# Gates of the latent projection two slots earlier, row slots planned by last use, dots moved between stages, and routing's last turns placed between value groups

## The reference

```python
h = modulate(rmsnorm(x, norm_w), shift, scale)
q, k, v, xr, yr = split(h @ w_in, 5 parts of 512)
att = neighbourhood_attention(q, k, v, k_ctx, v_ctx, rpb)      # latent; context: plain attention
xc  = centred_depthwise_conv(xr)                               # width 4
r, i = sigmoid(xc @ w_a + b_a), sigmoid(xc @ w_i + b_i)        # for each of two directions
a   = exp(8 * r * log_sigmoid(lam)); b = sqrt(1 - a*a) * (i * xc)
rg  = (scan_forward(a, b) + scan_backward(a, b)) * gelu(yr)    # RG-LRU
x   = x + gate_mix * (concat(att, rg) @ w_out)
h2  = modulate(rmsnorm(x, norm_ffn_w), shift2, scale2)
s   = (h2 @ w_q) . sub_keys            # 8 heads, two halves, 128 keys each
expert, g = top 16 of 16 x 16 candidates, softmax of their scores   # 128 (head, place) pairs a token
y   = sum over the 128: g * gelu(h2 . u[expert]) * v[expert]   # u, v: 16384 x 1024
out = rmsnorm(x + gate_ffn * y)
```

## Time and profile before

| | us |
|---|---|
| median of 3 executions | 3422.59 (3416.72 to 3429.27) |
| the profiled execution | 3423.91 |
| its span (first to last instruction) | 3422.1 |
| mean granted clock of PE | 0.962 |
| busy: PE, DVE, ACT, POOL | 3087.1, 2666.0, 1050.5, 1966.8 |
| latent projection | 358 to 652.5 |
| latent attention | 652.5 to 869.9 |
| latent output projection | 869.9 to 1024.8 |
| latent routing | 1024.8 to 1420.5 |
| place_weights | 1420.5 to 1637 |
| experts | 1637 to 3422 |

### The profile page before, as it was taken

How to read it: one execution, slowest core, us unless ns; L and a number is a source line. 1 busy time by engine, 2 the same in 40 slices (tenths; PEclk the granted TensorE clock), 3 DMA queues, 4 the chain that set the end, 5 groups by cost and what they waited for, 6 DMA issues and landing times.

```text
span 3422.1 us, 46361 instructions
## 1 busy us (share of the span) xinstructions
PE 3087.1 (90%) x15031; PEld 2030.5 (59%) x15031; DVE 2666.0 (78%) x5959; ACT 1050.5 (31%) x1886; POOL 1966.8 (57%) x1674
## 2 busy tenths in 40 slices
PE   6879899689899998677599999999999999999996
PEld 4647345456455444366365677776777766767774
DVE  2328788798577999699699788887878778877888
ACT  4731234366111111388211222222222222222222
POOL 0000466455335566453488777777777777777771
PEclk9989999799999999799799999999999999999998
DMA  9432688766867888799999999999999999999997
GB/s 338 167 110 95 215 267 277 233 213 219 321 227 259 297 290 303 272 337 390 343 366 384 411 412 412 412 411 411 412 411 412 411 411 411 412 412 412 411 412 303
DMA packets 374297, 1131.15 MB, mean 331 GB/s; under 512 B 32968, under 2 KB 99784, under 8 KB 374016
## 3 DMA queue, kind: packets, MB, share of 16 engines
q0 software_dynamic: 221184, 805.40, 62.0%
q1 hardware_dynamic: 144464, 316.41, 24.4%
q10 hardware_dynamic: 8496, 7.44, 0.7%
HBM read 1075.93 MB, written 53.19 MB: 330 GB/s over the span
## 4 chain that ended last, share of the span: by engine, by line
PE 23%; DMA 13%; POOL 6%; issue 6%; DVE 3%; ACT 0%; POOLq 0%; SPq 0%; DVEq 0%; ACTq 0%
DMA exp_value_row<-in_v_rows,exp_v_id 11%; PE exp_a_ps L2502 10%; PE exp_o_ps L2530 7%; PE exp_v_ps L2486 4%; POOL exp_value_row L2654 2%; PE exp_o_ps L2535 2%; POOL exp_more_row L2643 1%; POOL edge_u_raw L2643 1%; POOL edge_row L2643 1%; DMA exp_value_row<-in_u_rows,edge_id_and_dot 1%; DVE edge_u_raw L2708 0%; POOL exp_value_row L2643 0%; DMA exp_final_row<-scratch_x 0%; DVE exp_v_lo L2672 0%; DMA exp_out<-in_u_rows,edge_id_and_dot 0%
## 5 line engine op out<-in xcount | busy, mean ns | idle before, releaser
L403 POOL DMA_INDIRECT ahead_row<-in_u_rows,keep_tables x256 | 338.1, 1321 | 656.1 <-POOLq L102 364.1
L2654 POOL DMA_INDIRECT exp_value_row<-in_v_rows,exp_v_id x448 | 487.8, 1089 | 166.1 <-issue 136.0
L2502 PE MATMUL exp_a_ps<-exp_xT_hi,exp_u_hi 128*128 128x512 f32 x1024 | 411.0, 401 | 29.2 <-DVE exp_u_lo L2672 22.7
L2502 PE MATMUL exp_a_ps<-exp_xT_lo,exp_u_hi 128*128 128x512 f32 x1024 | 401.2, 392 | 0.0
L2502 PE MATMUL exp_a_ps<-exp_xT_hi,exp_u_lo 128*128 128x512 f32 x1024 | 400.3, 391 | 0.0
L413 DVE CUSTOM_DVE_ANT_0 ahead_row<-ahead_row,ahead_x 128x1024 f32<-128x1024 f32 x256 | 305.2, 1218 | 85.0 <-DMA ahead_row<-in_u_rows,keep_tables 84.5
L2789 DVE TENSOR_TENSOR keep_acc<-exp_o_ps,keep_acc 128x1024 f32<-128x1024 f32 x250 | 304.7, 1219 | 70.5 <-PE exp_o_ps L2530 53.1
L2585 ACT ACTIVATE exp_hidden<-exp_a_ps 128x512 f32<-128x512 f32 x128 | 76.6, 598 | 920.1 <-PE exp_a_ps L2502 920.1
L2643 POOL DMA_INDIRECT edge_row<-in_u_rows,edge_id_and_dot x224 | 292.8, 1307 | 103.1 <-POOL exp_v_id L2629 42.5
L2530 PE MATMUL exp_o_ps<-exp_v_hi,exp_w_hi 128*128 128x512 f32 x896 | 286.8, 401 | 5.1 <-DVE keep_acc L2838 5.1
L2530 PE MATMUL exp_o_ps<-exp_v_lo,exp_w_hi 128*128 128x512 f32 x896 | 281.7, 395 | 0.0
(11 more groups left out here) (446 smaller groups left out, 6230.3 us busy)
## 6 DMA issues: line engine op xcount, KB each, us to landing
exp_u_raw<-in_uT SPq DMA_DIRECT2D x126, 512.0 KB, 6.7
exp_v_raw<-in_v_rows SPq DMA_DIRECT2D x112, 512.0 KB, 6.7
exp_g_raw<-scratch_g SPq DMA_DIRECT2D x64, 512.0 KB, 7.9
scratch_g<-place_grid SPq DMA_DIRECT2D x3, 8192.0 KB, 51.1
proj_ctx_mod_slab<-in_w_mod SPq DMA_DIRECT2D x8, 2048.0 KB, 11.7
heads_early_room<-in_w_in SPq DMA_DIRECT2D x10, 1024.0 KB, 10.7
mod_slab<-in_w_mod SPq DMA_DIRECT2D x4, 2048.0 KB, 20.3
queries_slab<-in_w_q SPq DMA_DIRECT2D x4, 2048.0 KB, 24.5
```

Source lines behind the costliest of these rows:

```text
L403: nc.gpsimd.indirect_dma_start(out=ahead.row[:, n % KEY_RING, :], out_offset=None, in_=io["u_rows"], in_offset=bass.IndirectOffsetOnAxis(a ...
L2502: mm = nc.tensor.matmul(a_ps[e][:, :], u[part][:, e, k, :], xT[xp][:, k, :], start=(k == 0 and part == 0 and xp == 0), stop=(k == KD - 1 a ...
L2654: nc.gpsimd.indirect_dma_start(out=value_row[:, 4 * (j % 2) + t, :], out_offset=None, in_=io["v_rows"].rearrange("a b n -> (a b) n"), in_o ...
```

## The change

1. **Row slots.** `Ahead.rows` plans the slot of each row: the one whose last use is longest ago, of 4, or of up to 8 where more room is lent. In the projection two more rows lie in the parts of `v` that are filled last, for the first 104 units; in the output projection four more lie in `keep["acc"]`. `gather_keys` waits for the dot that last used the slot.
2. **Gates.** In the latent projection tile ct's gates begin at turn `FIRST_SLOT` = 6 (slot 6 of slab ct) instead of turn 8. PE and ACT follow one list of turns. ACT waits for dot 104 ahead of its V copy 4, the first into the lent room. ACT makes two of the four tiles of hT, DVE the other two.
3. **Dots.** Projection 136 gathers and 132 dots (8 first, then 3, 1, 4, 1, 1, 2 a direction), attention 64 gathers and 68 dots, output projection 56 dots (15 first, then 6 + 4 + 4).
4. **Bias.** SP loads pairs 0 and 1 at the end of the projection, when the last tile is done; in the attention it loads the context's values first and then pairs 2 and 3. 28 gathers stand ahead of the middle memsets, 40 before.
5. **Routing.** In the latent group's, two value groups, then the turns of one h2 tile, four times; one group; the identifiers' turns; the last three groups. h2 is turned into `q_ps[2]` and `q_ps[3]` and copied in halves. ACT's last `values_out` goes to the end, SP's second `values_store` behind the stores of h2.

The diff, cut to its core:

```diff
@@ class Ahead
+    def rows(self, units, more=(), until=0):
+        places = [self.row[:, n, :] for n in range(KEY_RING)] + list(more)
...
+        for at, n in enumerate(units):
+            usable = range(len(places) if at < until else KEY_RING)
+            s = min(usable, key=lambda p: last_use.get(p, -1))
...
+            if s in last_use:
+                self.freed_by[n] = last_use[s] + 1
+            last_use[s] = n
@@ def gather_keys
-    if n >= KEY_RING:
-        pool.wait_ge(ahead.dots, n - KEY_RING + 1)
+    row, landed = ahead.slot[n]
+    if n in ahead.freed_by:
+        pool.wait_ge(ahead.dots, ahead.freed_by[n])
@@ def projection_and_rg_lru
+    FIRST_SLOT = SLOTS_PER_SLAB if front is None else 2 * FRONT_TILES + 2
+    def tile_at(turn):
+        ct, step = divmod(turn - FIRST_SLOT, SLOTS_PER_SLAB)
+        return (ct, step) if 0 <= ct < RG_TILES else (None, None)
...
+        WIDE_DOTS = WIDE_RING_DOTS if units else 0
+        if units:
+            ahead.rows(units, [v[:, t:t + 2, :].rearrange("p i n -> p (i n)") for t in range(2 * FRONT_TILES, TILES_G, 2)], WIDE_DOTS)
...
+            if not context:
+                sp.wait_ge(tile_done, RG_TILES)
+                for q in range(EARLY_BIAS):
+                    load_bias(io, sp, early, bias_tiles(fused), q)
...
-                    if a:
-                        gate_products(a - 1, slot)
+                    gate_products(*tile_at(SLOTS_PER_SLAB * a + slot))
...
+                    if WIDE_DOTS and u == 2 * FRONT_TILES:
+                        act.wait_ge(ahead.dots, WIDE_DOTS)
...
+            for turn in range(0 if front is None else 2 * FRONT_TILES, SLOTS_PER_SLAB * (SLABS + 1)):
+                a, slot = divmod(turn, SLOTS_PER_SLAB)
+                ct, step = tile_at(turn)
+                gate_step(ct, step)
+                if a < SLABS:
+                    copy_features(a, slot)
+                else:
+                    copy_v(a, slot)
+                if step == SLOTS_PER_SLAB - 1:
+                    gelu(ct)
+            if not context:
+                act.wait_ge(tile_done, RG_TILES)
+                act.wait_ge(v_made, V_UNITS)
+                nc.scalar.activation(hT[:, 6:8, g.at:g.at + NT], fused[:, Y0 + 2:Y0 + 4, :], ACT.Copy)
...
-            dots_left = list(units)
+            dots_left = list(units[:-CARRIED_DOTS])
...
-                    dots(2)
+                    dots(3)
...
-                    dots(3)
+                    dots(4)
...
-            nc.vector.tensor_copy(hT[:, 4:8, g.at:g.at + NT], fused[:, Y0:Y0 + 4, :])
-DOTS_FIRST = 16
+            by_dve = 4 if context else 2
+            nc.vector.tensor_copy(hT[:, 4:4 + by_dve, g.at:g.at + NT], fused[:, Y0:Y0 + by_dve, :])
+DOTS_FIRST = 8
+CARRIED_DOTS = KEY_RING
+WIDE_RING_DOTS = 104
@@ def attention
-                for q in range(PAIRS):
-                    for half in range(2):
-                        sp.dma_start(bias[half * 64:half * 64 + 64, 2 * q:2 * q + 2, half:half + 15, :],
-                                     io["rel_bias"][:, 2 * q:2 * q + 2, :, :]).then_inc(bias_in[q], 16)
-                    if q == 0:
-                        sp.dma_start(v_ctx[:, :, :], io["v_ctx"].rearrange("l p n -> p l n")).then_inc(v_in, 16)
+                sp.dma_start(v_ctx[:, :, :], io["v_ctx"].rearrange("l p n -> p l n")).then_inc(v_in, 16)
+                for q in range(EARLY_BIAS, PAIRS):
+                    load_bias(io, sp, early, bias, q)
...
+                MIDDLE = len(units) // 2 - len(carried)
+                first_half, second_half = units[:MIDDLE], units[MIDDLE:]
@@ def out_projection
+            ahead.rows(units, [keep["acc"][:, n, :] for n in range(MORE_ROWS)], len(units))
...
-                    dots(5)
+                    dots(6)
...
-                        dots(3)
+                        dots(4)
@@ def routing
+        turned_ps = [h_ps[:, half * SLAB:(half + 1) * SLAB] if context else q_ps[2 + half] for half in range(2)]
...
+                values_store(val, sp, 0, scratch["ffn"][CTX.first])
             if not context:
                 for i in range(NG):
                     sp.wait_ge(h2_ready, i + 1)
                     sp.dma_start(scratch["h2"][i], h2[:, i % 2, :]).then_inc(h2_out[i % 2], 16)
+                values_store(val, sp, 1, scratch["ffn"][CTX.first + 1])
...
-            values(len(values_left))
-            if val:
-                pe.wait_ge(val.out_ready, CONTEXT_GATHER)
+            pe.wait_ge(q_ready, 4 * sum(len(parts_of(a)) for a in range(SLABS)))
             for i, t in enumerate(GATHERED):
                 if i:
                     pe.wait_ge(h2_ready, i)
+                values(2)
...
+            values(1)
...
             last.then_inc(ids_turned, 1)
+            values(len(values_left))
...
+            if val:
+                values_out(nc, val, act, 1, h_ps)
-PROJECTION_DOTS, ATTENTION_DOTS = 128, 80
+PROJECTION_DOTS, ATTENTION_DOTS = 136, 64
```

142 lines of the change are left out of this document (79 added, 63 removed).

## The result

The changed kernel takes 3404.28 us, median of 6 (3401.17 to 3407.83), against 3422.14 of the kernel before, median of 6 (3416.72 to 3429.27): a ratio of 0.9948, 95% interval 0.9935 to 0.996. That is 17.9 us less, where 33.5 were forecast; the time lies 0.7 us inside the upper end of the stated range. The profiled execution of the changed kernel took 3401.17 us, its span is 3399.4.

The account below looks back on a forecast made before the run. Experts were taken as DMA-bound, the latent stages as bound by their hand-overs. Projection -13.0, attention -11, output projection +1.5 and routing -11 gave -33.5: 3423.9 to 3390.4 us, by the median 3389; range 3378 to 3405.

Parts of the forecast that it names:

- The projection's work: Latent projection: earlier gates and six rows let DVE finish before PE; last copy at 639.1, 13.0 us less.
- Rival B: Latent projection: rows stay late, so the stage gains 5.2 us instead of 13.0; total 3397 us, chance 0.14.
- D: Projection rival: POOL gathers only between DVE's operations; total about 3421 us, slower from 2.32 dots a gather; chance 0.04.
- The projection's end: Hand-over to the attention: SP's wait for tile 3 and four bias loads cost nothing.
- The attention: Latent attention: bias waits 6.2, clock 3 and DVE-bound steps 2 give 11 us less; bounds 5 and 17.
- The bias waits: Attention's first steps: loading bias pairs 0 and 1 early removes waits of 4.75 and 1.45 us, 6.2 less.
- The clock: Attention's first four steps: a shorter PE pause keeps its clock up, 3 us less; range 0 to 7.6.
- The 12 steps bound by DVE: Attention after its first four steps: fewer dots give 0.2 us a step until PE takes over, 2 us less.
- the ring: Output projection: eight rows put four more gathers beside w_out, 0.4 us more; bounds 0 and 5.
- the dots: Output projection: eight more dots lie in DVE's slack, but one more precedes the last reciprocal, 1.1 us more.
- Routing: Latent routing: h2 turns and identifiers fit into PE's waits for gathers, 11 us less; bounds 8 and 14.
- Rival C: Small terms fail together: attention gains 8, routing 8, output projection loses 5; 3399.9 us, by the median 3399; chance 0.11.

Follow-up runs that it names:

- e9: Changed kernel with the latent projection's gates starting at turn 8 as before the change: projection 301.49 us against 288.10.
- e8: Changed kernel with four rows in the projection's ring throughout and no ACT wait for dot 104: projection 313.17 us against 288.10; execution 3427.88 us.
- e5: e2 with no row gathered in the projection for the attention (132 gathers there, 68 in the attention): projection 281.55 us, execution 3391.16 us.
- e2: Changed kernel with only bias pair 0 loaded early, after tile 1, and pairs 1 to 3 in the attention: projection 287.87 us against 288.10.
- e1: Changed kernel with all four bias pairs loaded in the attention, in the earlier order: projection 280.55 us against 288.10, attention 216.53 against 211.73.
- e7: Changed kernel with the attention's dots two, then three (six steps), then two a step, none in the last: attention 207.43 us against 211.73.
- e6: Changed kernel with the output projection's four more rows used only from its 16th gather on: output projection 155.05 us against 159.60.
- e10: Changed kernel with routing's order, turns and copies of the kernel before: routing 393.50 us against 384.64.

## Why the prediction was right and where it was wrong

**The projection's work: right.** The forecast put the last copy at 639.1, it is 638.15, in a stage that began 2.2 us earlier; from the stage's start the last copy comes 12.1 us sooner than before (forecast 13.0). The gates two slots earlier and the six rows are both needed (e9, e8), and DVE's last dot moves by nearly what the prediction gave: 12.7 us for 13.7, 23.7 for 23.4. The gates of tile 3 begin at 558.4, that is 560.6 with the 2.2. DVE ends tile 3 at 628.3 (forecast 632.4), its waits for rows are 15.3 us (forecast under 20), ACT's wait for dot 104 costs nothing. Rival B did not come, nor D: POOL's gathers took 1.41 us in the mean of the 194 into the old four rows (three stages), 1.47 for the projection's 136, far from the 2 that D needs with the 0.30 between them.

**The projection's end: the step that failed.** The text said of SP's wait and its four loads that nothing but the attention's loads stands behind them, "so it costs nothing here", and it gave the four carried gathers no price at all. The last of these goes out only when the last dots are done, and POOL's DRAIN at the block's end lasts until it has landed; SP's loads beside it make the landing later. From the last copy to the next stage it took 0.4 us before and takes 7.0 now, which is 6.6 of the 7.5 us that the stage fell short of its forecast; without the gathers the stage is 6.3 us shorter (e5 against e2), without the loads 7.6 (e1 against the changed kernel). The trace of before did show POOL's DRAIN at this place, ending 0.8 us behind the landing of its last gather (649.77 and 648.99), but the prediction did not read it, and DVE's copy hid it.

**The attention: one term over, one missing.** The bias waits gave what was forecast: the first four steps are 6.4 us shorter (forecast 6.2 for the bias and 3 for the clock). The clock gave nothing, and e5 with its short pause gained nothing more that shows. The doubt in the text, that PE's rests within these steps keep the clock down, fits that, but no run tested it. The 12 steps bound by DVE gave 2.4 (forecast 2). The end lost 3.2 us, which the text had not priced: the last step has three dots, as it had before, but the third now waits 2.99 us for its row in place of 1.39, and PE's clock falls with it. e7 shows that this end could even be 1.8 us shorter than before.

**The output projection: right mechanism, wrong size.** For the ring the text took 0.4 within bounds of 0 and 5, on the ground that the gathers' queue was full already, and 1.1 for the dots; the stage lost 4.4 with the clock, and e6, which keeps the dots, takes all of it back. So the ring's term was 4.4 and the dots' nothing.

**Routing: right.** -11.1 for -11, with the last group 3.3 us later (forecast 2, for the stores of h2; that it is the stores no run shows) and a shorter end than forecast: the store's landing and the hand-over took 3.5 us from SP's issue, not 4.5. By e10 8.9 is the change's; the other 2.2 go with PE's clock at the end of the stage in the kernel before, whose cause is open.

Rival C, the small terms failing together, is nearest: two of its three did, and the block's end came on top, in no rival. The changed kernel is 5 us above C's 3399.

**The range.** That 3404.28 lies in it is partly luck. The upper end is said to be B with C's half, but B's 3397 and half of C's 9.5 us come to about 3402, not 3405; the lower end, with half of the clock's 7.6, comes to about 3382, not 3378. And what brought the time up to the edge was the wait at the block's end, which neither B nor C holds.

## What to carry to other kernels

Before a gather by POOL is moved ahead of a hand-over between stages, read the DRAIN instructions at the block's end and look at whether the gather will have landed when the stage's last work ends, for the hand-over may wait for it. SP's loads were not waited for here, but beside a gather they delay its landing; a load that can go a tile earlier, or not until the next stage, avoided that. When a ring gets longer, ask what shares the DMA engines with it at that time: the same four rows cost 4 us beside w_out and were needed later in the same stage. A stage ends with the last link of its chain, so the last step of a loop should not carry filler work that may wait for a transfer.

## What the runs showed of the hardware

A gather by POOL that begins while DVE works mostly ends about 0.8 us after that DVE operation has ended (95 of 116 such gathers in the changed kernel's projection within 0.7 to 0.9): it takes 0.94 us when DVE rests, 1.68 in the earlier trace rows, and 1.98 in many others that begin just behind a boundary. A walk with this law, 1.14 us a dot and a landing of 4.15 us foretold that the last dot would move by 23.4 us with a ring of four; it moved by 23.7 (e8). It fits the lock that the Trainium skill tells of ("SBUF — State Buffer", section "A bandwidth-pool intuition that's wrong (but worth ruling out)"), where a transfer is blocked until DVE's operation has ended; its factor of five (620 to 3100 ns) is not seen here, where the longest gather of the projection took 2.75 us. That it is this lock was not tested.

POOL's DRAIN at a block's end lasted until 0.8 to 1.5 us after its last gather had landed, at the end of the projection in all fourteen profiles; it held the next stage up by 6.6 us in the changed kernel. SP's DRAIN took 0.37 us there, with four loads under way, and the last of them landed 0.9 us after the next stage's start.

After the same pause of 2.51 us PE's first four scores took 1.13 us in one run (e1, granted clock 1.00 in the 5 us from the first score on) and 2.08 in another (e5, 0.66). What the clock goes by is left open.
